# A hybrid attention encoder step: row tiles split in two-bank halves, and first projection products started on two row tiles

## What is computed

```python
def reference(x_prompt, x_sample, ..., norm_pre, norm_post, w_in, w_out, attn_sinks, rel_bias):
    hp = rms_norm(y_prompt, norm_pre[l])
    mp, st_p = mixers_prompt(hp, w_in[l], attn_sinks[l], rel_bias[l], slopes)
    y_prompt = y_prompt + rms_norm(jnp.einsum('btm,md->btd', mp, w_out[l]), norm_post[l])
    ...

def split_projection(h, w_in):
    p = jnp.einsum('btd,de->bte', h, w_in)
    ...
```

## Time and profile before

| | |
|---|---|
| median of 3 runs | 1940.13 us (1940.03 to 1941.39) |
| the profiled execution: its own time | 1939.99 us |
| its span in the profile | 1938.3 us |
| PE busy (matmuls) | 1907.4 us, 98% of the span |
| DVE busy | 1221.8 us, 63% |
| ACT busy | 667.4 us, 34% |
| groups L1194 to L1196 (first projection) | 3 x 2688 matmuls, 327, 321 and 321 ns each |

### The profile page before, as it was taken

The page is one execution under the profiler, slowest core; times in us unless marked ns, Lnnn a source line. Parts: engine busy times, 40 slices in busy tenths (PEclk is TensorE's granted clock), DMA queues, the critical chain, the costliest instruction groups (busy, mean ns, idle before and its releaser), DMA issues.

```text
span 1938.3 us, 31051 instructions
## 1 busy us (share of the span) xinstructions
PE 1907.4 (98%) x12604; PEld 1751.8 (90%) x12604; DVE 1221.8 (63%) x2176; ACT 667.4 (34%) x1257; POOL 51.9 (3%) x119
## 2 busy tenths in 40 slices
PE   5999999999999999999999999999999999999997
PEld 5999999999999999999999999999999988888886
DVE  7358677786877778554544454355525666766878
ACT  7124333343423334221222222233213354344453
POOL 3000000000000000000000000000000000000131
PEclk9999999999999999999999999999999999999999
DMA  6446777676777766666657657465446557555396
GB/s 245 117 115 140 156 154 166 144 147 153 151 156 155 170 139 144 157 136 134 154 117 154 147 129 143 104 145 123 107 97 145 131 195 284 192 175 187 122 257 226
DMA packets 880406, 301.05 MB, mean 155 GB/s; under 512 B 618504, under 2 KB 845592, under 8 KB 878968
## 3 DMA queue, kind: packets, MB, share of 16 engines
q1 hardware_dynamic: 877192, 290.35, 61.6%
q0 software_dynamic: 3072, 8.73, 2.2%
HBM read 210.45 MB, written 96.20 MB: 158 GB/s over the span
## 4 chain that ended last, share of the span: by engine, by line
PE 94%; DVE 4%; DMA 1%; issue 1%; ACT 0%; POOL 0%; DVEq 0%; SPq 0%; ACTq 0%; POOLq 0%
PE ps L1194 23%; PE ps L1195 22%; PE ps L1196 22%; PE ps L1405 4%; PE ps L1407 4%; PE ps L1406 4%; PE ps L1297 3%; PE ps L1376 3%; PE ps L1258 3%; PE ps L1347 3%; DVE arena L1738 1%; DVE act_lo L1745 1%; PE ps L1402 1%; PE ps L1401 1%; DMA arena<-in_x_prompt_dram 0%
## 5 line engine op out<-in xcount | busy, mean ns | idle before, releaser
L1194 PE MATMUL ps<-act_hi,w_hi 128*128 128x352 f32 x2688 | 877.8, 327 | 0.0
L1195 PE MATMUL ps<-act_lo,w_hi 128*128 128x352 f32 x2688 | 862.7, 321 | 0.0
L1196 PE MATMUL ps<-act_hi,w_lo 128*128 128x352 f32 x2688 | 862.6, 321 | 0.0
L1194 PEld LDWEIGHTS ps<-act_hi,w_hi 128*128 128x128 f32 x2688 | 504.6, 188 | 16.9 <-issue 14.0
L1195 PEld LDWEIGHTS ps<-act_lo,w_hi 128*128 128x128 f32 x2688 | 505.5, 188 | 0.0
L1196 PEld LDWEIGHTS ps<-act_hi,w_lo 128*128 128x128 f32 x2688 | 504.3, 188 | 0.0
L1508 ACT ACTIVATE w_hi<-w_raw 128x512 fp32r<-128x512 f32 x224 | 139.2, 623 | 344.7 <-DMA w_raw<-in_w_in_dram 344.6
L1753 DVE TENSOR_TENSOR w_lo<-w_raw,w_hi 128x512 fp32r<-128x512 f32 x224 | 150.5, 673 | 51.9 <-ACT w_hi L1508 51.7
L1575 ACT ACTIVATE arena<-arena,small 128x257 f32<-128x257 f32 (+6 forms) x180 | 101.2, 565 | 208.2 <-DVE small L1886 208.2
L2074 DVE STREAM_TRANSPOSE arena<-arena 128x1024 f32<-128x1024 f32 (+4 forms) x100 | 132.6, 1326 | 49.4 <-ACT arena L1696 48.6
L1696 ACT ACTIVATE arena<-arena 128x1024 f32<-128x1024 f32 (+1 forms) x60 | 61.1, 1018 | 251.8 <-DVE arena L1860 251.8
(11 more groups left out here) (183 smaller groups left out, 2097.3 us busy)
## 6 DMA issues: line engine op xcount, KB each, us to landing
w_raw<-in_w_in_dram SPq DMA_DIRECT2D x176, 256.0 KB, 3.3
weight_scratch<-arena SPq DMA_DIRECT2D x216, 128.0 KB, 3.5
arena<-weight_scratch SPq DMA_DIRECT2D x54, 512.0 KB, 4.6
b_out<-in_w_out_dram SPq DMA_DIRECT2D x72, 256.0 KB, 3.3
w_raw<-in_w_out_dram SPq DMA_DIRECT2D x70, 256.0 KB, 2.6
w_raw<-in_w_in_dram SPq DMA_DIRECT2D x96, 128.0 KB, 3.1
weight_scratch<-arena SPq DMA_DIRECT2D x80, 132.0 KB, 4.0
arena<-weight_scratch SPq DMA_DIRECT2D x40, 256.0 KB, 3.4
```

The source lines that it names most:

```text
L1194: mm(bank(g, GN), wh, ah, start=(k == 0), stop=False)
L1195: mm(bank(g, GN), wh, al, start=False, stop=False)
L1196: last = mm(bank(g, GN), wl, ah, start=False, stop=(k == KT - 1))
```

## The change

Three things are done, all in the row stage.

1. For tiles 0 to 7, ACT and DVE handle two PSUM banks in one instruction of 1024 columns (`x_high_two`, and the first branch of `x_low`). Semaphores count by two, so their totals stay. Tile 8 keeps the old form.
2. The split of the first weight tile follows tile 1 and not tile 2. On ACT it stands behind the second half of tile 1. On DVE the first two pieces stand ahead of `x_low(1)`, the other two behind it.
3. The first products are cut by columns. Group 0 is done as columns 0 to 255 (the first two row tiles) and 256 to 351, group 1 as 0 to 159 and 160 to 351. The table `EARLY` says what follows which tile; group 2 is as before.

```diff
+        def two_banks(h):
+            return ps[:, 512 * (X + 2 * h):512 * (X + 2 * h) + 1024].rearrange("p (k t) -> p k t", k=8)
...
-            def first_project(g, *quarters):
-                pe.wait_ge(x_lo, 4 * (3 * g + 3))
+            def first_product(g, q, a, b):
+                for kk in range(4):
+                    k = 4 * q + kk
+                    wh, wl = w_hi[:, q, P * kk:P * kk + P], w_lo[:, q, P * kk:P * kk + P]
+                    ah, al = act_hi[:, k, GN * g + a:GN * g + b], act_lo[:, k, GN * g + a:GN * g + b]
+                    out = bank(g, b - a, P, a)
+                    mm(out, wh, ah, start=(k == 0 and a == 0), stop=False, skip_group_check=True)
+                    mm(out, wh, al, start=False, stop=False, skip_group_check=True)
+                    last = mm(out, wl, ah, start=False, stop=(k == KT - 1), skip_group_check=True)
+                return last
+
+            def first_project(g, a, b, *quarters):
+                end = GN * g + b
+                pe.wait_ge(x_lo, 4 * min((end - 1) // P + 1, TT + 1))
                 for q in quarters:
                     pe.wait_ge(lo_made, q + 1)
-                    last = product(g, q)
-                    if q == 3:
+                    last = first_product(g, q, a, b)
+                    if q == 3 and b == GN:
                         last.then_inc(proj_done, 1)
...
+            EARLY = {2: [(0, 0, 2 * P, 0, 1)], 3: [(0, 0, 2 * P, 2, 3), (0, 2 * P, GN, 0, 1, 2, 3)],
+                     4: [(1, 0, 4 * P - GN, 0, 1)], 5: [(1, 0, 4 * P - GN, 2, 3)],
+                     6: [(1, 4 * P - GN, GN, 0, 1)], 7: [(1, 4 * P - GN, GN, 2, 3)]}
...
-                if t >= 3:
-                    first_project(t // 3 - 1, *((0,), (1, 2), (3,))[t % 3])
-            first_project(GROUPS - 1, 0, 1, 2, 3)
+                for part in EARLY.get(t, ()):
+                    first_project(*part)
+            first_project(GROUPS - 1, 0, GN, 0, 1, 2, 3)
...
+            def x_high_two(t, h):
+                act.wait_ge(xt_done, 4 * t + 2 * h + 2)
+                fn(act_hi[:, 8 * h:8 * h + 8, P * t:P * t + P], two_banks(h), ACT.Copy).then_inc(x_hi, 2)
...
-                x_high(t, 0)
-                x_high(t, 1)
+                x_high_two(t, 0)
                 if t < TT - 1:
                     x_guess(t + 2)
-                x_high(t, 2)
-                x_high(t, 3)
-                if t == 2:
+                x_high_two(t, 1)
+                if t == 1:
                     for q in range(4):
                         high(0, q)
...
+                if t < TT:
+                    for h in (0, 1):
+                        dve.wait_ge(x_hi, 4 * t + 2 * h + 2)
+                        v.tensor_tensor(act_lo[:, 8 * h:8 * h + 8, P * t:P * t + P], two_banks(h),
+                                        act_hi[:, 8 * h:8 * h + 8, P * t:P * t + P].bitcast(F32),
+                                        ALU.subtract).then_inc(x_lo, 2)
+                    return
...
+                if t == 1:
+                    low(0)
+                    low(1)
                 x_low(t)
-                if t == 2:
-                    for q in range(4):
-                        low(q)
+                if t == 1:
+                    low(2)
+                    low(3)
```

More of the change, by code:

```diff
@@ L1209, in project @@
                     last.then_inc(piece_used, 1)
-            def first_project(g, *quarters):
-                pe.wait_ge(x_lo, 4 * (3 * g + 3))
+            def first_product(g, q, a, b):
[11 more added lines that the diff above has]
+                pe.wait_ge(x_lo, 4 * min((end - 1) // P + 1, TT + 1))
                 for q in quarters:
                     pe.wait_ge(lo_made, q + 1)
-                    last = product(g, q)
-                    if q == 3:
+                    last = first_product(g, q, a, b)
+                    if q == 3 and b == GN:
                         last.then_inc(proj_done, 1)
-                    elif g == GROUPS - 1:
+                    elif q < 3 and g == GROUPS - 1:
                         last.then_inc(piece_used, 1)
+            EARLY = {2: [(0, 0, 2 * P, 0, 1)], 3: [(0, 0, 2 * P, 2, 3), (0, 2 * P, GN, 0, 1, 2, 3)],
+                     4: [(1, 0, 4 * P - GN, 0, 1)], 5: [(1, 0, 4 * P - GN, 2, 3)],
+                     6: [(1, 4 * P - GN, GN, 0, 1)], 7: [(1, 4 * P - GN, GN, 2, 3)]}
             def set_ready(key):
@@ L1513, in _ @@
             for t in range(TT + 1):
+                if t == TT:
+                    for g in range(4):
+                        x_high(t, g)
+                    continue
                 if t < TT - 1:
                     x_squares(t + 2)
-                x_high(t, 0)
-                x_high(t, 1)
+                x_high_two(t, 0)
                 if t < TT - 1:
                     x_guess(t + 2)
-                x_high(t, 2)
-                x_high(t, 3)
-                if t == 2:
+                x_high_two(t, 1)
+                if t == 1:
                     for q in range(4):
```

## The result

The changed kernel took 1949.19 us, the median of four runs (1948.17 to 1950.23; a fifth, of 5881.09 us, is left out as disturbed), beside 1941.39 us for the kernel before (five runs, 1940.03 to 1942.64): a ratio of 1.0040 [1.0028, 1.0053], +7.8 us. It is slower, by more than the 0.2% that can be told; the forecast was 1946.5 in a range of 1943.0 to 1949.8. The profiled execution of the changed kernel took 1949.05 us with a span of 1947.3, against 1939.99 and 1938.3 before: +9.0 us of span.

The account below looks back on a forecast made before the run. PE, 98% busy, was taken as the bound, so the time follows group 2's start: 57.34 to 63.3 us gives +6.0, plus 0.4 for the clock, 1946.4, to the median 1946.5; range 1943.0 to 1949.8.

Parts of the forecast that it names:

- Step 1: Two banks per instruction: DVE's second halves wait about 0.4 us per tile for ACT's copy; period 4.65 to about 5.0.
- Step 2: Weights behind tile 1: DVE idle from 22.0 to 24.0 us for the first weight piece; PE's tile 2 at 26.6.
- Step 3: Cut products: narrow matmuls on PE cost 0.11 us each whatever their width; tile 4 at 42.5, group 2 at 63.3.
- The bounds, 0.05 and 0.16: Limits for a narrow matmul's cost on PE: 0.05 to 0.09 us by columns alone, 0.16 as a matmul of today.
- its own 0.4 us for the clock: PE idle from 21.6 to 26.6 us may run tile 2 and 12 products at 1.2 GHz; half of 0.9 us counted.
- The rival of nearly free short products: Short products cost only columns, PE never the bound: +3.2 us, 1943.3; chance 0.14, shared with smaller waits.
- the rival of two cycles a column: Narrow fp32r products on PE cost 0.11 to 0.17 us, like plain f32 transposes: +9.1 us, 1949.1; chance 0.07.
- The sum: Group 2's start on PE moves from 57.34 to 63.3 us, +6.0, plus 0.4 for the clock: 1946.4 us.
- the projection behind the row stage would not change: Sign: the prediction is wrong if the projection behind the row stage changes; its idle time should stay where it is.
- slow short products: Rival: short fp32r products on PE cost more than their columns; +9.1 us, or +12.4 at 0.16 each; chance 0.07.

Follow-up runs that it names:

- part 1 alone: The kernel before with only the two-bank instructions on ACT and DVE added: 1943.79 us, ratio 1.0015.
- the second trace: The changed kernel profiled once more with nothing moved: 1948.8 us, one run.
- parts 2 and 3 alone: The kernel before with only the weight split moved behind tile 1 (1942.81 us, ratio 1.0011), and with only the cut first products (1948.06 us, ratio 1.0040).
- part 3 alone: The kernel before with only the first products cut by columns and the table `EARLY`: 1948.06 us, ratio 1.0040.

## Why the prediction was right

**Step 1** was right: the waits of 0.40 us are in the changed kernel and in part 1 alone, the period is 5.02 for 5.0, and with the guess behind both halves the waits are gone. Part 1 alone costs 3.0 us at the start of group 2 where 2.9 was expected.

**Step 2** was right: the wait for `w_hi` is 1.98 us and ends at 23.98 (forecast 2.0 and 24.0), tile 2 starts at 26.56 (26.6). Tile 3 starts at 33.12, 0.7 later than the 32.4 of the text, and most of it is the clock: tile 2's transposes took 3.65 us, and in the second trace, with 3.32, tile 3 starts at 32.60. The first product starts at 29.86 and not at 28.6, so next to nothing was gained in time there.

**Step 3** was right in its mechanism and its price. The pitch of 96 columns is 0.1115 us for an estimate of 0.11; tile 4 starts at 43.02 (42.5), DVE waits till 45.31 (44.6), group 2 starts at 63.80 (63.3). The bounds, 0.05 and 0.16, were far apart, and the row to choose by was the earlier trace rows, the spacing of weight loads that wait for nothing. The rule of the Trainium skill that was weighed ("TensorE: Matmul & The Clock Gate", Back-to-back issue gap), 81 ns for pairs of 128 columns, does not hold for this kernel's fp32r matmuls: 0.111 to 0.112 us for 88, 96, 160, 176 and 192 columns. Another section of that page of the Trainium skill (LDWEIGHTS) has a load take its columns over 1.2 GHz, by which 128 columns take an estimated 107 ns. The traces agree within 5 ns at full clock; at the lower clock they don't, the pitch of 88 and 96 columns being 0.213 us. The sum that the prediction gave for 81 ns, +4.6 us, also left out its own 0.4 us for the clock; with it, it is +5.0. The rival of nearly free short products fell with the pitch, and the rival of two cycles a column with it: 192 columns cost as much as 88.

**The sum** was short by 2.6 us of the profiled difference of 9.0: 0.1 at the start of group 2, 1.7 in group 2 and 0.8 in the output stage. The term that was mis-sized is the clock: it stood at 0.4, half of an early loss of 0.9. By the trace it is 0.7 us at tile 3, of which 0.5 reach the start of group 2 (in the second trace, without most of that loss, group 2 starts at 63.28, as the sum without the term has it). Inside this term two sizes were off against each other: a transpose at the lower clock costs 0.109 us more and not 0.08, and three or four products met it and not 12. The term has nothing for group 2, where the clock cost 1.7 us: the forecast had PE wait for tile 8 and did not ask what clock it would go on at. That the projection behind the row stage would not change, which the prediction had made a sign of being wrong, held only between group 2 and the output stage. The 0.8 us of the output stage are half a longer wait for DVE; that stage moves by -0.2 to +1.1 us in the experiments too, and why is open.

The measured 1949.19 us is 2.7 above the forecast and 0.6 under the upper end of the range. Of the 2.7, 1.3 are the kernel before, whose median of five runs is 1941.39 and not the 1940.13 of three. By the medians the difference is 7.8 us, 1.4 above the forecast. The range reached so far up for slow short products, not for the clock: that it held this miss as well is in part luck.

**What is open** is what exactly brings the clock down. It is low behind waits of 4.6 us (parts 2 and 3 alone). It also fell in a run of 88 columns per load without any wait, and in one of 96 in one trace out of six; with 176 columns per load, in one trace, it did not. In group 2 it fell in both traces of the changed kernel and in none of four variants: with part 3 alone and with the guess behind both halves PE waits only the last 0.69 us there, with a quarter behind tile 8 it waits longer but has products in between, and with group 1 uncut neither short products nor a wait stand ahead. So the waits of the changed kernel are part of the cause, but not their length alone. Whether it is the columns, the loads, or what stood before them was not told apart.

## What to carry to other kernels

Before a matmul is cut, compare its columns with its weight load: here anything from 88 to 192 columns costs 0.11 us, so cutting 352 into 256 and 96 adds 0.07 us each time, and can pay only where PE would stand idle. When two instructions are merged, ask for the second half's input and the first half's release: both come later, and 0.09 us of saved overhead a tile was paid with 0.4 us of waiting. And when an engine gets one more wait ahead of a list in strict order, follow everything behind it, the clock of the engine that is made to wait included.

## What the runs showed of the hardware

- The granted clock fell to 0.50 on a PE that had not been idle: in 88-column matmuls at 63.7 us, where it stayed for 34 us, and, in one trace of six, in 96-column ones at 40.4 us, where it stayed for 6.8.
- The place of a low stretch is not fixed by the instructions. The kernel before and its variants with group 2 cut have the same lists up to 57 us; the record is low from 27.3 to 30.8 us in the first, from 22.8 to 26.2 with four cuts, and from 18.3 to 21.7 and 28.6 to 32.0 with two.
- At the lower clock the pitch is 0.213 us for 88, 96 and 256 columns, 0.29 for 352, against 0.111, 0.1115, 0.119 and 0.159 at full clock: short matmuls take twice as long there too.
- The record of the granted clock does not show every low stretch. In the changed kernel it reads 1.00 from 27 to 28 us (columns as in the stretches of that kernel above) while tile 2's 16 transposes take 3.65 us, against 1.91 in tile 3. The duration of a row is the surer sign:

```profile
27.00:28.00 1.00, 1.00 (x7) 1.00 (x6) 1.00 (x2) 0.40 (x2) 0.52 (x1) 1.00 0.00 0
```
- POOL's variance, an instruction of 0.19 us at 12.84 with no scaling beside it, takes until DVE's scaling ends when it starts during one: 1.67 us from 20.39 to 22.06 in the changed kernel, beside a scaling from 19.66 to 22.00.
